# Expert block of a mixture-of-experts kernel: the next block's input transposes stand between the up and the gate products, in place of behind the gate products

## The chip, the cores and the metric

The kernel runs on one core of a Trainium2 chip. The metric is the device time of one execution in microseconds (us); lower is better. The engines are named as the profile names them: PE (TensorE, with PEld for its weight loads), DVE (VectorE), ACT (ScalarE), POOL (GpSimd) and SP (SyncE, which issues most of the DMAs).

## The reference

One layer of a streaming encoder on 2048 prompt tokens and 32 sample tokens of width 1024: a joint projection, a convolution group beside a stick-breaking attention group, an output projection, and then a mixture of 32 experts in 4 groups, of which each token uses two. The change lies in the experts, whose part of the reference is this:

```
def expert_block(args):
    xe, e = args                      # 128 rows of tokens, one expert
    return (jax.nn.silu(xe @ w_g[e]) * (xe @ w_u[e])) @ w_d[e]
yb = lax.map(expert_block, (xb, block_e))
out = zeros.at[row_tok].add(yb * row_w[:, None])
```

xe is 128x1024, w_g and w_u are 1024x512, w_d is 512x1024. Each expert has at least one block of 128 rows; the data of this case gives 46 blocks over 32 experts.

## The kernel before

The program has three stages, each with its own semaphores and a barrier behind it: projection and convolution (names p1_), attention and output projection with the router, and the experts (names p3_, function phase_moe). Only the third is touched. It begins some 1335 us into the span; its blocks run from 1369 us to 2191 us.

All matrices are float32. For precision each operand is kept as a high part (fp32r, written by ACT with a copy) and a low part (the rest, written by DVE with a subtraction), and each product is made of three matmuls: hi x hi, hi x w_lo, lo x w_hi. So one k-tile of 128 rows costs three matmuls.

Work of PE in one block b, in program order (PE runs its instructions in order; each engine has its own stream, ordered by the semaphores that are named):

- up: 8 k-tiles x 3 matmuls of 512 columns into the PSUM tile p_up (L2310, helper `hidden`).
- gate, first half of the columns: 8 x 3 matmuls of 256 columns into p_gp; then five k-tiles of the second half (15 matmuls).
- transpose_h(b, 0): two 128x128 transposes (matmuls against the identity, L2289) of the first half of h, into p_htp.
- the last three k-tiles of the second half of gate (9 matmuls).
- transpose_x(b + 1): eight 128x128 transposes (L2282) of the next block's rows p_xg, into p_xtp.
- down: k-tile 0 of the first 512 output columns (3 matmuls of 512 columns, p_dp, L2301), transpose_h(b, 1) (two transposes), then 21 more matmuls of down.

What stands beside it: ACT's `gate(b, k)` (L2233) makes silu of half k of gate as soon as it is complete (g_done), DVE's `gated(b, k)` (L2441) multiplies it by up into h (h_done), and transpose_h(b, k) waits for that. ACT's `h_hi(b, k)` (L2238) and DVE's `h_rest(b, k)` (L2445) make the high and low part of the transposed h (hl_done), and `down` waits for hl_done[0] before its first matmul and for hl_done[1] before its 13th. ACT's `x_hi(b + 1)` (L2228) and DVE's `x_rest(b + 1)` (L2433) do the same with the next block's x; the next block's up waits for them. ACT's order in a block is: up's weights, gate(b, 0), two weight pieces, h_hi(b, 0), gate(b, 1), x_hi(b + 1), h_hi(b, 1), weights, output of down (L2253), weights. The order of DVE is likewise written out by hand in `block_of`.

Between these, ACT (L2223) and DVE (L2428) split the next expert's weights, which SP loads into a ring of 16 pieces of 512 KB (L2178); this is only done in an expert's last block. POOL gathers the rows of block b + 2 by an indirect DMA into p_xg (L2494), once transpose_x(b + 1) has read the buffer (semaphore xt_ps), and then adds the output of block b into y_out by another (L2504). transpose_x(b) waits for the gather's landing (`gathered`) and for `xl_done`.

The waits at the head of down, in PE's stream, are these:

```
weights(e, 3)
pe.wait_ge(hl_done[0], b + 1)
pe.wait_ge(yo_done, b)
down(0, (0,))
transpose_h(b, 1)
```

Of the kernel before, what the change touches and what calls it, by code (L numbers as in the profile page):

```python
# [2076 lines left out]
def phase_moe(nc, io, scr, picks):  # L2077
# [6 lines left out]
    with ExitStack() as ctx:  # L2084
# [85 lines left out]
        @block.sync  # L2170
        def _(sp):
            def load(i, a):
                for p, src in enumerate(pieces(i * 4 + a)):
                    n = a * PIECES + p
                    if not (isinstance(i, int) and n < RING):
                        sp.wait_ge(wlo_done, i * (4 * PIECES) + n - RING + 1)
                    dst = raw[:, n % RING, :]
                    sp.dma_start(dst.rearrange("p (k f) -> p k f", k=2) if p < 2 * KT // 2 else dst,  # L2178
                                 src).then_inc(raw_in[n % RING], 16)

            sp.wait_ge(zero_yo, 1)
            sp.dma_start(scr["h2"][PAD:ROWS, :], yo[:, :]).then_inc(zeroed, 16)
            sp.dma_start(io["y_out"][PAD:ROWS, :], yo[:, :]).then_inc(zeroed, 16)
            for a in range(4):
                load(0, a)
            with sp.Fori(1, NE // 4) as i:
                for a in range(4):
                    load(i, a)
            sp.wait_ge(zeroed, 32)
# [77 lines left out]
        @block.tensor  # L2267
        def _(pe):
            for n, (k, r) in enumerate(choices):
                m = DEC if ORDER[r] == PT else P  # L2270
                if n in pool_rows:
                    pe.wait_ge(row_in, pool_rows.index(n) + 1)
                pe.wait_ge(spread_in, n + 1)
                pe.matmul(up[:, 0:2 * NBL], homes[n % HOMES][0:m, :],  # L2274
                          in_col[0:m, n % RS, :, :].rearrange("p v b -> p (v b)"),
                          start=(n == 0), stop=(n == len(choices) - 1)).then_inc(spread, 1)

            def transpose_x(b):
                pe.wait_ge(gathered, b * 16)
                pe.wait_ge(xl_done, b)  # L2280
                for k in range(KT):
                    last = pe.transpose(xtp[:, k, :], xg[:, k * P:(k + 1) * P], ident[:, :])  # L2282
                last.then_inc(xt_ps, 1)

            def transpose_h(b, k):
                pe.wait_ge(h_done[k], b + 1)
                for x in range(2):
                    f = 2 * k + x
                    last = pe.transpose(h_cols[k][:, x, :], h[:, f * P:(f + 1) * P], ident[:, :])  # L2289
                last.then_inc(ht_ps[k], 1)  # L2290

            def weights(e, groups):

                pe.wait_ge(whi_done, e * PIECES + groups * 4)
                pe.wait_ge(wlo_done, e * PIECES + groups * 4)

            def down(c, fs):

                for f in fs:
                    for n, (ha, wa) in enumerate(((ht_hi, w_hi), (ht_hi, w_lo), (ht_lo, w_hi))):  # L2300
                        last = pe.matmul(dp[:, c, :], ha[:, f, :], wa[2][:, f, c * 512:(c + 1) * 512],  # L2301
                                         start=(f == 0 and n == 0), stop=(f == FT - 1 and n == 2))
                return last

            def hidden(dst, group, lo, hi, ks):

                for k in ks:
                    for n, (xa, wa) in enumerate(((xt_hi, w_hi), (xt_hi, w_lo), (xt_lo, w_hi))):
                        at = k % 2 * FF
                        last = pe.matmul(dst, xa[:, k, :], wa[group][:, k // 2, at + lo:at + hi],  # L2310
                                         start=(k == 0 and n == 0), stop=(k == KT - 1 and n == 2))
                return last

            for done in (xt_ps, up_done, *g_done, *ht_ps, d_done):
                pe.sem_inc(done, 1)
            def keep_warm(count):

                for _ in range(count):
                    pe.matmul(dp[:, 0, :], w_hi[0][:, 0, 0:P], w_hi[0][:, 0, 0:512], start=True, stop=True)  # L2319

            pe.wait_ge(whi_done, 1)
            keep_warm(22)
            pe.wait_ge(ident_done, 2)
            transpose_x(1)
            keep_warm(8)
            pe.wait_ge(table_done, 1)
            with pe.Fori(0, NE) as e:
                start, end = (pe.value_load(table[0:1, x, bass.ds(e, 1)], min_val=1, max_val=NBL - 2) for x in range(2))
                with pe.Fori(start, end + 1) as b:
                    pe.wait_ge(xh_done, b + 1)  # L2330
                    pe.wait_ge(xl_done, b + 1)
                    weights(e, 1)
                    pe.wait_ge(h_done[1], b)
                    hidden(up[:, :], 0, 0, FF, range(KT)).then_inc(up_done, 1)
                    weights(e, 2)
                    hidden(gp[:, 0, 0:HF], 1, 0, HF, range(KT)).then_inc(g_done[0], 1)
                    hidden(gp[:, 1, 0:HF], 1, HF, FF, range(5))
                    transpose_h(b, 0)
                    hidden(gp[:, 1, 0:HF], 1, HF, FF, range(5, KT)).then_inc(g_done[1], 1)
                    transpose_x(b + 1)  # L2340
                    weights(e, 3)
                    pe.wait_ge(hl_done[0], b + 1)
                    pe.wait_ge(yo_done, b)
                    down(0, (0,))
                    transpose_h(b, 1)
                    down(0, (1,))
                    down(1, (0, 1))
                    pe.wait_ge(hl_done[1], b + 1)
                    down(0, (2, 3))
                    down(1, (2, 3)).then_inc(d_done, 1)  # L2350
# [249 lines left out]
```

## Time and profile before

| | |
|---|---|
| median of 3 runs | 2202.96 us (2202.63 to 2206.08) |
| the profiled execution, its own time | 2202.57 us |
| its span, first to last instruction | 2200.8 us |
| mean granted TensorE clock | 0.977 |
| PE / PEld busy | 2088.1 us (95%) / 1771.5 us (80%) |
| DVE / ACT / POOL busy | 1623.4 / 1260.0 / 806.9 us |
| expert blocks | 46, from 1368.9 us to 2191 us |

The busy time of an engine sums its instructions. PE's matmuls are pipelined and the ends are modelled, so two neighbours overlap in the rows; the distance from start to start says what one costs. A chain of waits follows the work that ended last back from the end. PEldq is PE's sequencer, with its own instructions: semaphore waits (EVENT_SEMAPHORE), register operations and branches. Clock 1.00 is the full 2.4 GHz.

### The profile page before, as it was taken

Reading aid. Unit: us, or ns where it says so; the run is one execution under the profiler, and the core shown is the slowest. Engines: PE = TensorE matmul, PEld = TensorE weight load, DVE = VectorE, ACT = ScalarE, POOL = GpSimd, SP = SyncE. Lnnn points to the kernel's source line nnn. Section 1 sums busy time; section 2 is a strip of 40 time slices with the busy share of each in tenths; the row PEclk is TensorE's granted clock in tenths of the full one; section 3 lists DMA queues with packets and bytes.
Section 4 is the critical chain, followed back from the end, with each engine's and each line's share of the span. In section 5 each row is a group of like instructions: output and inputs, shape, how many; then the busy total and the mean of one; then the engine's idle time right before and its main releaser. Section 6 shows DMA issues by size and latency. Waiting matters only on the chain. (4 is left out here: it accounts for less than half of the span.)

```text
span 2200.8 us, 40164 instructions
## 1 busy us (share of the span) xinstructions
PE 2088.1 (95%) x13505; PEld 1771.5 (80%) x13506; DVE 1623.4 (74%) x2083; ACT 1260.0 (57%) x2200; POOL 806.9 (37%) x689
## 2 busy tenths in 40 slices
PE   8999999995899999899999895999999999999998
PEld 6888888884687887678787774888888888888887
DVE  3799999984777667867878967969698556556644
ACT  5322433335677777866676643768588555456533
POOL 1111544553566654545545435222222222222221
PEclk9999999996999999999999996999999999999999
DMA  7553344334333242333222117989899968767852
GB/s 228 186 191 134 118 128 159 120 106 144 114 117 109 80 131 81 108 105 116 80 73 92 54 70 258 361 281 372 308 357 373 329 197 282 228 198 264 285 172 35
DMA packets 211517, 393.17 MB, mean 179 GB/s; under 512 B 54749, under 2 KB 81757, under 8 KB 211389
## 3 DMA queue, kind: packets, MB, share of 16 engines
q1 hardware_dynamic: 197853, 357.42, 47.1%
q0 software_dynamic: 13536, 34.12, 6.8%
q8 instruction: 72, 1.18, 0.2%
q14 instruction: 56, 0.46, 0.1%
HBM read 315.42 MB, written 91.23 MB: 185 GB/s over the span
## 5 line engine op out<-in xcount | busy, mean ns | idle before, releaser
L2428 DVE TENSOR_TENSOR p_w_lo<-p_raw,p_w_hi 128x1024 fp32r<-128x1024 f32 (+1 forms) x260 | 439.5, 1728 | 150.5 <-ACT p_w_hi L2223 149.9
L2051 POOL TENSOR_TENSOR p_wgt<-p_wgt,p_past 128x1024 f32<-128x1024 f32 (+4 forms) x166 | 308.5, 1859 | 347.2 <-DVE p_past L1929 347.1
L2223 ACT ACTIVATE p_w_hi<-p_raw 128x2048 fp32r<-128x2048 f32 (+1 forms) x198 | 361.8, 1859 | 84.0 <-PE p_up L2310 67.3
L762 DVE SCALAR_TENSOR_TENSOR p_ut<-p_ut,p_cw 128x512 f32<-128x512 f32 (+1 forms) x480 | 329.2, 762 | 0.0
L1929 DVE TENSOR_TENSOR_SCAN p_past<-p_keep,p_past,p_one 128x513 f32<-128x513 f32 (+1 forms) x196 | 225.9, 1193 | 75.3 <-ACT p_keep L1746 73.3
L1746 ACT ACTIVATE p_keep<-p_zp 128x512 f32<-128x512 f32 (+3 forms) x326 | 158.8, 547 | 119.2 <-PE p_zp L1620 106.5
L2310 PE MATMUL p_gp<-p_w_hi,p_xt_hi 128*128 128x256 f32 x736 | 210.4, 286 | 0.0
L436 PE MATMUL p_pj<-p_w_hi,p_xt_hi 128*128 128x512 f32 x512 | 205.2, 401 | 4.2 <-DVE p_xt_lo L738 2.4
L2310 PE MATMUL p_gp<-p_w_lo,p_xt_hi 128*128 128x256 f32 x736 | 206.5, 281 | 0.0
L2310 PE MATMUL p_gp<-p_w_hi,p_xt_lo 128*128 128x256 f32 x736 | 206.4, 280 | 0.0
L436 PE MATMUL p_pj<-p_w_hi,p_xt_lo 128*128 128x512 f32 x512 | 200.6, 392 | 0.0
L436 PE MATMUL p_pj<-p_w_lo,p_xt_hi 128*128 128x512 f32 x512 | 200.2, 391 | 0.0
L2492 POOL COPY p_at_g<-p_slots 128x1 int32 (+1 forms) x47 | 30.8, 656 | 384.8 <-PE p_xtp L2282 382.3
L1759 ACT ACTIVATE p_at<-p_tp 128x512 f32<-128x512 f32 (+3 forms) x261 | 134.2, 564 | 60.3 <-PE p_tp L1630 59.7
L2504 POOL DMA_INDIRECT y_out<-p_yo,p_at_s x47 | 87.8, 1868 | 205.6 <-ACT p_yo L2253 204.7
L1751 ACT ACTIVATE p_wgt<-p_zp 128x512 f32<-128x512 f32 (+3 forms) x326 | 160.3, 562 | 0.0
L1630 PE MATMUL p_tp<-p_ident,p_wgt 128*128 128x128 f32 x1106 | 150.6, 275 | 6.7 <-DVE p_at L1942 5.7
L1658 PE MATMUL p_op<-p_at,p_v 128*64 128x128 f32 x2176 | 156.0, 282 | 0.0
L2301 PE MATMUL p_dp<-p_w_hi,p_ht_hi 128*128 128x512 f32 x368 | 151.1, 411 | 0.4 <-DVE p_ht_lo L2445 0.4
L1929 DVE TENSOR_TENSOR_SCAN p_past<-p_keep,p_one 128x385 f32<-128x385 f32 (+3 forms) x130 | 114.0, 918 | 49.7 <-ACT p_keep L1746 42.8
L2301 PE MATMUL p_dp<-p_w_lo,p_ht_hi 128*128 128x512 f32 x368 | 143.7, 391 | 0.0
L1630 PEld LDWEIGHTS p_tp<-p_ident,p_wgt 128*128 128x128 f32 x1106 | 128.9, 141 | 18.3 <-DVE p_at L1942 6.9
(309 smaller groups left out, 4975.6 us busy)
## 6 DMA issues: line engine op xcount, KB each, us to landing
p_raw<-in_w_up SPq DMA_DIRECT2D x128, 512.0 KB
p_raw<-in_w_gate SPq DMA_DIRECT2D x128, 512.0 KB
p_raw<-in_w_down SPq DMA_DIRECT2D x128, 512.0 KB
wide_raw<-in_w_in SPq DMA_DIRECT2D x56, 256.0 KB, 3.8
wide_raw<-in_x SPq DMA_DIRECT2D x17, 512.0 KB
scr_y<-wide_raw SPq DMA_DIRECT2D x17, 512.0 KB, 3.1
wide_raw<-scr_y SPq DMA_DIRECT2D x17, 512.0 KB
y_out<-wide_raw SPq DMA_DIRECT2D x17, 512.0 KB, 2.9
```

The source lines that it names most:

```text
L436: last = pe.matmul(pj_of(n), xa[:, b, k, :], wa[place[c]][:, k, :], start=(m == 0), stop=(m == 3 * KT - 1))
L762: dve.scalar_tensor_tensor(dst, src, cw[:, a, j:j + 1], dst, ALU.mult, ALU.add).then_inc(tap_done, 1)
L1630: end = pe.transpose(tp[:, n % 2, b * P:(b + 1) * P], wgt[:, u % NW, x * HW + b * P:x * HW + (b + 1) * P], ident[:, :])
L1658: end = pe.matmul(op[x * HD:(x + 1) * HD, pair * P:(pair + 1) * P], v_sb[:, key_slot(g, kt), h * HD:(h + 1) * HD], at[:, (base[u] + x) % N ...
L1746: act.activation(keep_rows[:, u % NK, x, HW - w:HW], zp[:, (base[u] + x) % NZ, 0:w], ACT.Sigmoid, scale=-SCALE).then_inc(keep_done, 1)
L1751: act.activation(wgt[:, u % NW, x * HW:x * HW + w], zp[:, (base[u] + x) % NZ, 0:w], ACT.Sigmoid, scale=SCALE).then_inc(sig_done, 1)
L1929: end = dve.tensor_tensor_scan(past[:, u % NP, to + w + 1:to:-1], src, one[:, 0:1].broadcast_to([P, w + 1]), past[:, (u - 1) % NP, to + 1: ...
L2051: pool.tensor_tensor(mine, mine, past_rows[:, u % NP, 0:n, 2:2 + w], ALU.mult).then_inc(a_done, 1)
L2223: act.activation(part(w_hi, p, wide), raw[:, n % RING:n % RING + wide, :], ACT.Copy).then_inc(whi_done, wide)
L2301: last = pe.matmul(dp[:, c, :], ha[:, f, :], wa[2][:, f, c * 512:(c + 1) * 512], start=(f == 0 and n == 0), stop=(f == FT - 1 and n == 2))
L2310: last = pe.matmul(dst, xa[:, k, :], wa[group][:, k // 2, at + lo:at + hi], start=(k == 0 and n == 0), stop=(k == KT - 1 and n == 2))
L2428: dve.tensor_tensor(part(w_lo, p, wide), raw[:, n % RING:n % RING + wide, :], part(w_hi, p, wide).bitcast(F32), ALU.subtract).then_inc(wlo ...
```

## The change

transpose_x(b + 1) is moved in PE's stream from behind the last gate product to the place between the last up product and the wait for the gate weights. Nothing else is edited: the streams of ACT, DVE, POOL and SP are as they were, and every semaphore is waited for and raised by the same instructions.

```
                     hidden(up[:, :], 0, 0, FF, range(KT)).then_inc(up_done, 1)
+                    transpose_x(b + 1)
                     weights(e, 2)
                     hidden(gp[:, 0, 0:HF], 1, 0, HF, range(KT)).then_inc(g_done[0], 1)
                     hidden(gp[:, 1, 0:HF], 1, HF, FF, range(5))
                     transpose_h(b, 0)
                     hidden(gp[:, 1, 0:HF], 1, HF, FF, range(5, KT)).then_inc(g_done[1], 1)
-                    transpose_x(b + 1)
                     weights(e, 3)
                     pe.wait_ge(hl_done[0], b + 1)
```

## Rows read from the trace of the kernel before

**Rows 1.** The page: the span in 40 equal slices, PE, granted clock and DMA.

```profile
PE   8999999995899999899999895999999999999998
PEclk9999999996999999999999996999999999999999
DMA  7553344334333242333222117989899968767852
```

**Rows 2.** Windows of three blocks: us, busy of each engine, clock, DMA share, GB/s.

```profile
1386.80:1404.66 17.86, 17.86 (x109) 15.91 (x108) 16.26 (x14) 14.40 (x12) 4.96 (x4) 1.00 0.99 324
...
1690.42:1708.96 18.54, 18.10 (x110) 15.94 (x108) 16.17 (x14) 14.64 (x12) 3.67 (x4) 1.00 1.03 367
```

**Rows 3.** The chain that ended last, through one block: start, us, what.

```profile
1637.01 5.44 PE p_up L2310 x24
1642.45 4.59 PE p_gp L2310 x39
1647.04 0.22 PE p_htp L2289 x2
1647.26 1.04 PE p_gp L2310 x9
1648.30 0.87 PE p_xtp L2282 x8
1649.17 0.70 PE p_dp L2301 x3
1649.87 0.22 PE p_gp L2289 x2
1650.09 4.78 PE p_dp L2301 x21
```

**Rows 4.** Timeline of the same block: start, us, engine, instruction.

```profile
1636.84 0.39 PE L2310 MATMUL p_up<-p_w_hi,p_xt_hi 128*128 128x512 f32 x1
...
1639.26 2.00 POOL L2504 DMA_INDIRECT y_out<-p_yo,p_at_s  x1 [3.85 <-ACT p_yo L2253]
...
1647.40 0.37 ACT L2238 ACTIVATE p_ht_hi<-p_htp 128x256 fp32r<-128x256 f32 x1
1647.80 0.43 DVE L2445 TENSOR_TENSOR p_ht_lo<-p_htp,p_ht_hi 128x256 fp32r<-128x256 f32 x1 [0.44 <-ACT p_ht_hi L2238]
1648.02 0.28 PE L2310 MATMUL p_gp<-p_w_hi,p_xt_lo 128*128 128x256 f32 x1
1648.14 1.03 PE L2282 MATMUL p_xtp<-p_ident,p_xg 128*128 128x128 f32 x8
1648.34 0.38 ACT L2233 ACTIVATE p_sg<-p_gp 128x256 f32<-128x256 f32 x1 [0.57 <-PE p_gp L2310]
1648.75 0.42 DVE L2441 TENSOR_TENSOR p_h<-p_up,p_sg 128x256 f32<-128x256 f32 x1 [0.53 <-ACT p_sg L2233]
1648.93 0.48 PE L2301 MATMUL p_dp<-p_w_hi,p_ht_hi 128*128 128x512 f32 x1
1649.43 0.93 POOL L2492 COPY p_at_g<-p_slots 128x1 int32 x1 [8.17 <-PE p_xtp L2282]
1649.71 0.38 PE L2289 MATMUL p_gp<-p_ident,p_h 128*128 128x128 f32 x2
1651.23 1.07 POOL L2494 DMA_INDIRECT p_xg<-scr_h,p_at_g  x1 [0.87 <-POOL p_at_g L2492]
...
1654.70 0.39 PE L2310 MATMUL p_up<-p_w_hi,p_xt_hi 128*128 128x512 f32 x1
```

**Rows 5.** Timeline of the one block whose down products waited.

```profile
1702.52 0.42 DVE L2445 TENSOR_TENSOR p_ht_lo<-p_htp,p_ht_hi 128x256 fp32r<-128x256 f32 x1 [1.32 <-ACT p_ht_hi L2238]
1703.20 0.47 PE L2301 MATMUL p_dp<-p_w_hi,p_ht_hi 128*128 128x512 f32 x1 [0.44 <-DVE p_ht_lo L2445]
1703.96 0.38 PE L2289 MATMUL p_gp<-p_ident,p_h 128*128 128x128 f32 x2
```

**Rows 6.** PE's sequencer in lines 2342 and 2343, 1700 to 1705 us.

```profile
L2342 PEldq EVENT_SEMAPHORE  x1: 51/51/51, 1703.0 to 1703.0; - x1
L2343 PEldq EVENT_SEMAPHORE  x1: 51/51/51, 1703.1 to 1703.1; - x1
```

**Rows 7.** Timeline, attention stage: transposes that waited for a DVE copy.

```profile
554.66 0.41 DVE L1942 COPY p_at<-p_tp 128x256 f32<-128x256 f32 x1
555.13 0.44 PE L1630 MATMUL p_tp<-p_ident,p_wgt 128*128 128x128 f32 x2 [0.29 <-DVE p_at L1942]
```

**Rows 8.** Who waited for whom, 1360 to 2200 us: us, times, longest.

```profile
POOL p_at_g L2492 <- PE p_xtp L2282: 382.3, 46, 10.5
```

**Rows 9.** PE's sequencer at the end of one block, lines 2329 and 2333.

```profile
L2329 PEldq FUSED_REGOPS  x2: 37/39/41, 1651.1 to 1653.4; - x2
L2333 PEldq EVENT_SEMAPHORE  x1: 51/51/51, 1653.7 to 1653.7; - x1
```

**Rows 10.** The instructions of line 2282, all blocks: ns min/median/max.

```profile
L2282 PE MATMUL p_xtp<-p_ident,p_xg x376: 270/272/421, 1364.5 to 2185.4; 128*128 128x128 f32 x188
```

**Rows 11.** DMA queue of the gathers and adds, 1657 to 1658 us: packets, MB, share.

```profile
q0 software_dynamic: 41, 0.09, 24.1%
```

More of the change, by code:

```diff
@@ L2334, in _ @@
                     hidden(up[:, :], 0, 0, FF, range(KT)).then_inc(up_done, 1)
+                    transpose_x(b + 1)
                     weights(e, 2)
@@ L2339, in _ @@
                     hidden(gp[:, 1, 0:HF], 1, HF, FF, range(5, KT)).then_inc(g_done[1], 1)
-                    transpose_x(b + 1)
                     weights(e, 3)
```

## Prediction

> **What bounds the kernel now.** I read the page first, for where PE has holes: in the expert stage, the last third of the slices, PE is busy throughout and its clock is granted in full, while the DMA engines are nearly full up to about 1700 us and less so behind [rows 1]. Then the windows of single blocks: a block lasts 17.86 us and PE is busy for all of it; DVE is busy for 16.2 us, ACT for 14.4 [rows 2]. Then the chain of waits, which settles the bound: it runs through PE alone, from up to gate to transposes to down, and the pieces sum to 5.44 + 4.59 + 0.22 + 1.04 + 0.87 + 0.70 + 0.22 + 4.78 = 17.86 us [rows 3]. So PE never waits in a normal block, and anything that PE does no sooner or that makes it wait is paid once per block, 46 times. One block lasts 18.54 us, 0.68 more; there a weight piece came late and the low part of h with it, and down's first product waited [rows 2, 5].
>
> The last view is the timeline around the edit, because a PE that never waits may do so only since the eight transposes cover something. They do. The last gate product starts at 1648.02. The low part of the transposed h, for which down waits, is done at 1647.80 + 0.43 = 1648.23, which is 0.21 behind that start; the second half of h, for which the next transposes of h wait, is done at 1648.75 + 0.42 = 1649.17, which is 1.15 behind it. The transposes of x fill PE from 1648.14 to 1648.93, so both are ready when PE comes to them, at 1648.93 and 1649.71 [rows 4].
>
> **What the edit removes, adds and moves.** It removes nothing. It moves eight transposes, the two waits ahead of them, and the release that POOL and ACT take from them.
>
> (1) The price of the eight in their new place. Start to start they take 0.79 us (1648.14 to 1648.93) [rows 4], and the chain, which also counts what the first product behind them loses, gives 0.87 [rows 3]. The two transposes of h inside the gate products cost 0.22 in the chain, 0.11 each, so eight ahead of gate products cost 0.88 by the same measure [rows 3]. I take 0.87; 0.79 is the low end. All that stands behind them in the block, gate, silu and h, comes 0.87 later.
>
> A rule speaks against this price. The Trainium skill, page "TensorE: Matmul & The Clock Gate", section "Part 4: PE-mode transpose", gives about 275 ns for a transpose in a kernel; by it the eight would cost 2.2 us in a place where nothing overlaps them, and the kernel would take some 61 us more than by my sum. This trace shows the same length for one transpose, 272 ns at the median, but eight of them in 1.03 us, since they are pipelined [rows 4, 10]; the spacing decides.
>
> (2) What is uncovered. Measured from the start of the last gate product, the transposes of h's second half start now at 1649.71 - 1648.02 = 1.69 us. Without the eight, down would start at 0.12 and these transposes 0.78 behind it (1648.93 to 1649.71), at 0.90 [rows 4]. Two chains hold them back, and neither moves with the eight, for both start from gate products:
>
> - down's first product waits for the low part of h, done at 0.21. Where PE did wait for it, the product started 0.26 behind the end (1702.52 + 0.42 = 1702.94 to 1703.20), as two semaphore instructions of PE's sequencer still stood between [rows 5, 6]. I take 0.25: start at 0.46, and the transposes of h 0.76 behind (1703.20 to 1703.96) [rows 5], at 1.22.
> - the transposes of h wait for h, done at 1.15. How fast that wait lets go is not shown for this line. The nearest row is a transpose that waited for a DVE copy: done at 555.07, started at 555.13, 0.06 [rows 7]. That gives 1.21. The far end is the 0.26 of down's wait: 1.41. I take 0.06, since line 2286 has no semaphore instruction of its own in the sequencer, unlike lines 2342 and 2343 [rows 6]: the wait sits on the transpose itself, as in the attention stage.
>
> The two chains end together, so one stall of about 0.31 us in all (1.22 less 0.90), most of it ahead of down's first product. That the pipe is empty when the transposes start costs a little: two took 0.44 after a wait where two in a flow take 0.38 [rows 4, 7]; I count half of the 0.06, 0.03, as in most blocks this second wait is nearly nil.
>
> (3) The sum for a block: 0.87 + 1.215 - 1.69 + 0.03 = +0.425 us, and 46 x 0.425 = 19.6 us. (Of the 0.425, 0.31 is the stall and 0.03 the refill; 0.08 is what the eight cost beyond their spacing, which the product behind them pays: now gate's first one, while down's first pays as much for the empty pipe.) The block of 18.54 us had a wait of its own in the same place, 0.68 us, from a weight piece that was late. In the new kernel 18 blocks before it are longer by 0.4 us each while the loads are the same, so I count that wait as gone: 19.6 - 0.7 = 18.9. On the profiled execution, span 2200.8 becomes 2219.7 us; what lies around the span (1.8 us) stays, and the median of the runs, 0.4 us above the profiled time, becomes 2202.96 + 18.9 = 2221.9 us.
>
> (4) The rest comes to nothing, with this cover. ACT's high part of the next x starts as soon as silu of the second half is done, no longer after a wait, and its 1.03 us still end before h's second half is transposed, so h_hi(b, 1) isn't later. DVE's low part of that half is done about 1.5 us behind the start of its transposes (1.22 us of weight work stand before it), plus 0.25 for the release, and down needs it 0.14 + 9 x 0.227 = 2.2 us behind them: 0.4 us of slack, and a third stall if that goes. The next x is split 2 us before the block ends. POOL takes its release for the next gather some 5 us earlier in the block, at about 6.5 us instead of 12.6 (1649.43 less the block's start of 1636.8) [rows 4, 8], and its add of the last output is off the engine by then (1639.26 + 2.00, 4.4 us into the block); so the gather and the copy behind it only come earlier. The gather must now have landed 5.7 us into the next block, not 11.3: issue to need stays at 15 us, while the gather issued at 1651.23 shows its packets until 1658 [rows 4, 11]. In the first block alone the issue doesn't move and the cover shrinks to some 6 us, with 4 needed. SP isn't passed; its ring is freed by DVE's weight work, whose pace is set elsewhere.
>
> **Rivals.**
>
> - *The release of h is slow too.* If the transposes of h start 0.26 behind h, they start at 1.41 and the block costs 0.87 + 1.41 - 1.69 + 0.06 = 0.65 us; 46 x 0.65 = 29.9, with the late weight still there: 2233 us. For it: it is the only release of PE in this stage that the trace shows. Against: the missing semaphore instruction.
> - *The sequencer loses its lead.* At an expert's end it needs 2.6 us for its loop (1651.1 to 1653.7) and is done 1.0 us before the next up's first product at 1654.70 [rows 4, 9]. It now gets past down's wait 0.87 later while the block ends 0.43 later, so its lead sinks to about 0.55. If its issue is slower than I take it, each 0.1 us beyond costs 3.2 us over 32 experts; 0.5 beyond gives 2238 us. The Trainium skill, page "Runtime: NRT & Kernel Launch", section "Instruction fetch mechanics", says that a taken branch can force an instruction fetch that stalls; no row here shows such a stall between blocks.
> - *Not slower: the transposes are cheap behind up.* A 512-column product takes 5.44 / 24 = 0.227 us, so 128 columns at that pace take 0.057, and eight transposes 0.45. Then the block costs 0.45 + 1.215 - 1.69 = -0.02 us and the time is 2202 us, the same as now. It decides once the eight cost less than 0.48 us. Against: in all three places of the block they cost 0.11 each [rows 3].
> - *The gather is late.* If landing took 15 us and not 7, each us beyond would cost 46 us. It needs DMA queues much fuller than the trace shows, and I put no size in the range for it.
>
> **How the numbers follow.** The forecast (stall of 0.3 us and nothing hidden) has 0.79; slow release 0.09; sequencer 0.05; cheap transposes 0.03; late gather 0.04. The forecast's own bounds: with the eight at 0.79 and no refill, 0.79 + 1.21 - 1.69 = 0.31 us, 14.3 - 0.7 = 13.6, 2216.5; with the refill in full and the late weight kept, 0.46 x 46 = 21.2, 2224. The range of 8 in 10 takes in most of the slow release: 2214 to 2230 us. Faster or slower by under 0.2% (4.4 us) can't be told from no change. Faster 0.01 (transposes cheaper still, or the late weight's 0.7 us and more), same 0.03, slower 0.96.
>
> **What the profile after would show.** A block period of about 18.28 us. PE idle ahead of p_dp, put down to DVE p_ht_lo, in all 46 blocks, some 0.1 to 0.3 us each, where one stood before; next to none or under 0.1 ahead of the transposes of h. Eight transposes between up and gate, 0.87 us in the chain; ACT p_xt_hi no longer waiting for p_xtp. POOL's copy at 6.5 us into the block. No wait at p_xtp for the gather, and the block near 1690 us like the others. I'm wrong if the period stays at 17.86, which would mean that the eight lost most of their price, or if it is 18.5 or more, where the row ahead of p_gp (L2289) will say whether it was the release of h, or an idle PE ahead of up the sequencer.

## The result and the profile after

The changed kernel is slower: median of six runs 2215.66 us (2213.93 to 2223.40) against 2202.80 us (2199.69 to 2206.08) of six runs of the kernel before. The ratio is 1.0065, 95% interval 1.0046 to 1.0084, so 10.1 to 18.5 us more, 12.9 by the medians. The profiled execution has a span of 2214.1 us, 13.3 more than before.

The chain of waits through one block of the changed kernel, start, us and what; the rows answer to [rows 3]:

```profile
1639.64 5.44 PE p_up L2310 x24
1645.08 0.87 PE p_xtp L2282 x8
1645.95 4.44 PE p_gp L2310 x39
1650.39 0.22 PE p_htp L2289 x2
1650.61 1.06 PE p_gp L2310 x9
1651.67 0.23 issue
1651.90 0.94 PE p_dp L2301 x3
1652.84 0.22 PE p_gp L2289 x2
1653.06 4.78 PE p_dp L2301 x21
```

The block lasts 18.20 us against 17.86. Three things differ, read against [rows 3]. The eight transposes stand ahead of gate at the same price, 0.87. Behind gate there is now "issue" (time in which the chain finds no instruction at work; the timeline below shows PE waiting there for the low part of h), and the three down products behind it have grown from 0.70 to 0.94: together 0.47 us that were not there. And, not foreseen, the 39 gate products take 4.44 in place of 4.59.

The timeline of the same block, behind gate; it answers to [rows 4]:

```profile
1651.22 0.42 DVE L2445 TENSOR_TENSOR p_ht_lo<-p_htp,p_ht_hi 128x256 fp32r<-128x256 f32 x1 [0.52 <-ACT p_ht_hi L2238]
...
1651.39 0.28 PE L2310 MATMUL p_gp<-p_w_hi,p_xt_lo 128*128 128x256 f32 x1
...
1651.71 0.38 ACT L2233 ACTIVATE p_sg<-p_gp 128x256 f32<-128x256 f32 x1 [0.52 <-PE p_gp L2310]
1651.90 0.47 PE L2301 MATMUL p_dp<-p_w_hi,p_ht_hi 128*128 128x512 f32 x1 [0.23 <-DVE p_ht_lo L2445]
...
1652.12 0.43 DVE L2441 TENSOR_TENSOR p_h<-p_up,p_sg 128x256 f32<-128x256 f32 x1 [0.48 <-ACT p_sg L2233]
...
1652.67 0.39 PE L2289 MATMUL p_gp<-p_ident,p_h 128*128 128x128 f32 x2
```

From the start of the last gate product (1651.39): the low part of h is done at 0.25, down starts at 0.51, h's second half is done at 1.16, its transposes start at 1.28. PE now has nothing of its own to do between the last gate product and the first wait. Who waited for whom, 1360 us to the end (us, times, longest), answers to [rows 8]:

```profile
POOL y_out L2504 <- ACT p_yo L2253: 425.1, 46, 11.7
...
POOL p_at_g L2492 <- PE p_xtp L2282: 115.2, 46, 4.7
...
PEld p_dp L2301 <- issue: 15.8, 46, 0.4
PEld p_gp L2289 <- DVE p_h L2441: 12.1, 46, 0.4
...
PE p_dp L2301 <- DVE p_ht_lo L2445: 6.2, 27, 0.3
```

PE's weight loads wait in all 46 blocks at both places, where before down's products had waited once [rows 5]. POOL's wait for the transposes fell from 382 to 115 us, while its wait for the block's output rose from 205 to 425 us and that for the landing of its last add from 5 to 66: the gather is issued earlier and nothing comes of it.

Windows of two blocks of the changed kernel, which answer to [rows 2] (us, busy of PE, PEld, DVE, ACT and POOL, clock, DMA share, GB/s):

```profile
1639.47:1657.67 18.20, 17.98 (x109) 15.73 (x108) 16.17 (x14) 14.40 (x12) 4.64 (x4) 1.00 1.04 382
1493.61:1511.97 18.36, 18.20 (x110) 15.88 (x108) 16.16 (x14) 14.40 (x12) 4.62 (x4) 1.00 1.03 362
```

The granted clock is full (1.00) in both, as before. But blocks come in two lengths. Of the 45 distances between the first up products of neighbouring blocks, 40 are 18.18 to 18.27 us and five 18.36 to 18.38; in those five the 39 gate products took 4.60 us. The chain through one of them:

```profile
1500.09 4.60 PE p_gp L2310 x39
...
1505.96 0.16 issue
1506.12 0.94 PE p_dp L2301 x3
1507.06 0.27 PE p_gp L2289 x2
```

The mean is 18.23 us, 0.354 more than the 17.876 of before (820.37 and 804.42 us over 45 blocks), where 17.876 has the late weight piece of [rows 5] in it. That is 16.3 us over 46 blocks; 3.0 us of it the profiled execution got back ahead of the change, since its first block happened to begin at 1365.91 us and not at 1368.90.

### The profile page after: what moved, and what is told of

Same layout as the page of the kernel before. It is cut to its first block and busy times, and to the rows that moved or that the text cites. A ratio compares the mean times of both kernels' runs of the same rounds, so it can differ in the third digit from the quotient of the medians.

```text
span 2214.1 us, 40164 instructions
## 1 busy us (share of the span) xinstructions
PE 2095.7 (95%) x13505; PEld 1763.0 (80%) x13506; DVE 1622.7 (73%) x2083; ACT 1258.7 (57%) x2200; POOL 807.3 (36%) x689
## 5 line engine op out<-in xcount | busy, mean ns | idle before, releaser
L2310 PE MATMUL p_up<-p_w_hi,p_xt_hi 128*128 128x512 f32 x368 | 143.2, 389 | 0.9 <-DVE p_xt_lo L2433 0.9
L2301 PE MATMUL p_dp<-p_w_hi,p_ht_lo 128*128 128x512 f32 x368 | 144.0, 391 | 0.0
```

## The experiments

The theory, called the cover theory: the transposes behind gate hid two chains, and what is lost is that cover. The rival, called the place theory: transposes cost more between up and gate. In every kernel of these only PE's stream is edited, and the edits are shown against the changed kernel; "period" is the distance from one block's first up product to the next one's. `transpose_x` has got a range of k-tiles; the waits go with its first part, the signal with its last. Where only one execution of a kernel was taken, its period is what is compared, and not its time.

**Four ahead, four behind.**

```
                     hidden(up[:, :], 0, 0, FF, range(KT)).then_inc(up_done, 1)
-                    transpose_x(b + 1)
+                    transpose_x(b + 1, 0, 4, False)
...
                     hidden(gp[:, 1, 0:HF], 1, HF, FF, range(5, KT)).then_inc(g_done[1], 1)
+                    transpose_x(b + 1, 4, KT)
```

> Four of the eight transposes of x between up and gate, four behind gate. Cover theory (the change costs because the two waits, for the low part of h and for h, are no longer covered; they need about 0.4 us of other work behind the last gate product): four transposes behind gate are 0.43 us, so down's first product starts 0.55 us behind the last gate product, no wait shows, and the block period is 17.86 us as before the change, or about 17.70 if the quicker pace of the gate products (0.1135 in place of 0.118 us each) that stands in 40 blocks of the changed kernel comes with any transposes ahead of gate. Time 2203 us, or 2196. Place theory (transposes ahead of gate cost more than behind it, about 1.2 us for eight): half of the loss is left, 18.04 us, time 2209.

Measured: 2205.60 us against 2204.69, ratio 1.0008 (0.9997 to 1.0019). The mean period of the profiled execution is 17.85 us, and the blocks come in two lengths. The chain through two neighbours:

```profile
1601.53 5.44 PE p_up L2312 x24
...
1607.40 4.44 PE p_gp L2312 x39
...
1613.13 0.44 PE p_xtp L2283 x4
1613.56 0.72 PE p_dp L2303 x3
...
1625.18 4.60 PE p_gp L2312 x39
```

Four transposes behind gate are enough to take "issue" out of the chain, and down's first three products are back at 0.7. The period is 17.76 to 17.79 where the 39 gate products take 4.44 us, and 17.91 to 17.94 where they take 4.60. Of the loss of 0.50 us that a block with the long gate has in the changed kernel, 0.07 is left here and not half, so the place theory falls; that the mean period is back at that of before is in part owed to the short gate.

**Six ahead, two behind** (the same edit with 6).

> Six transposes ahead of gate, two behind. Cover theory: the two behind fill 0.22 us of a wait of 0.39, so 0.17 us of waiting is left: period 18.21 - 0.22 = 17.99 us, time about 2206. Place theory: three quarters of the loss, 18.12 us, time 2212.

Measured: 2210.89 us against 2204.69, ratio 1.0032 (1.0021 to 1.0044); the mean period is 18.035, with most blocks at 17.96 to 18.08 and the rest at 18.13 to 18.16. The 17.99 of the cover theory is that of a block with the short gate. The profiled execution took 2206.69 us, about the forecast, though 10 of its 45 blocks had the long gate; it is the fastest of seven, and the median lies 5 us over what I gave. The kernel before stood 2 us higher here as well (2204.69); what the slower executions did otherwise no trace shows.

**The eight in both places.**

```
                     hidden(up[:, :], 0, 0, FF, range(KT)).then_inc(up_done, 1)
-                    transpose_x(b + 1)
+                    transpose_x(b + 1, 0, KT, False)
...
                     hidden(gp[:, 1, 0:HF], 1, HF, FF, range(5, KT)).then_inc(g_done[1], 1)
+                    transpose_x(b + 1)
```

> The eight transposes are done twice, ahead of gate (extra work, its result is overwritten) and behind gate. It gives the price of eight in the new place with the cover kept. Cover theory: no wait; period 17.86 + 0.74 = 18.60 us with the quick gate pace, 17.86 + 0.90 = 18.76 with the slow one; 34 to 41 us over before in all. Place theory: 17.86 + 1.2 = 19.06.

Measured: one execution, 2245.53 us; the period is 18.79 or 18.80 us in every block but the first, 0.93 over the 17.86 of before. The chain:

```profile
1600.83 0.87 PE p_xtp L2283 x8
1601.71 4.60 PE p_gp L2312 x39
...
1607.59 0.88 PE p_xtp L2283 x8
```

No wait, and the same eight transposes cost 0.87 in one place and 0.88 in the other. That is the price of the place by itself: nothing to choose. The other 0.06 of the 0.93 lies in products: gate's last one came 0.90 later and not 0.87, and from the transposes of h to the block's end it took 5.03 us and not 4.99; why, no run shows.

**No transposes but the first block's.** This kernel leaves out the transposes of x for all later blocks, so each computes with the first block's x.

```
-                    transpose_x(b + 1)
+                    pe.wait_ge(gathered, (b + 1) * 16)
+                    pe.wait_ge(xl_done, b + 1)
+                    pe.sem_inc(xt_ps, 1)
```

> Leaves out the transposes of x of all blocks but the first (each block computes with the x of the first one); their waits and their signal stand in the new place. Cover theory: gate loses the 0.79 us that the eight took ahead of it, and the waits behind gate stay as in the changed kernel, 0.38 us in all: period about 18.21 - 0.79 = 17.42, so that leaving out 0.87 us of PE work gains only 0.44 against before. Place theory: no waits that matter, 17.86 - 0.87 = 16.99.

Measured: one execution, 2189.09 us; period 17.44 to 17.51, once 17.59 and once 20.02 (a late weight piece at 1700 us). The chain behind gate:

```profile
1592.49 0.16 issue
1592.65 0.94 PE p_dp L2301 x3
1593.59 0.28 PE p_gp L2289 x2
```

The waits of the changed kernel are here without any transpose ahead of gate. (0.16 and not 0.23 of issue: the low part of h is done 0.18 behind the start of the last gate product here, and not 0.25.) The 39 gate products took 4.59 to 4.60 us in every block. Taking 0.87 us of work off PE shortened the block by 0.40: the rest of the eight's price had been cover.

**Three ahead, five behind.**

> Three transposes ahead of gate, five behind. Cover theory: 0.54 us behind gate cover the wait in full and no instruction of PE is released by another engine; period 17.86 us, or 17.93 if the slow pace behind transposes costs 0.07. On the pace of the gate products, two theories: it is quick (0.1135 us a product) wherever transposes stand ahead of gate: then quick in all or many blocks, 17.77 us; or it can only change where PE is released by another engine's semaphore somewhere in the block AND transposes stand ahead of gate (as the double transposes, with no wait, were slow in every block, and the kernel without transposes, with waits, too): then slow in all blocks, 17.93.

Measured: one execution, 2200.95 us. Cover: as expected, no wait in a normal block. Pace: both theories fell. The first 17 blocks behind the first lasted 17.76 or 17.77 us each; the 19th lasted 21.97, as weights came late and PE waited; behind it nearly all blocks lasted 17.89 to 17.93. The chain before and behind that wait:

```profile
1601.40 4.44 PE p_gp L2312 x39
...
1926.78 4.60 PE p_gp L2312 x39
```

So transposes ahead of gate don't shorten it by themselves, and it can be short with no wait in the block. Here the pace was kept for many blocks; the first block behind the long wait was still short, and from the next one on nearly all were long, so that the wait changed the pace is not shown.

**Five ahead, three behind.**

> Five ahead, three behind. Cover theory: 0.33 us behind gate leave 0.06 us of the wait uncovered: period 17.77 + 0.06 = 17.83 us in blocks with the quick gate pace, 18.00 in those with the slow one; with more than half of the blocks quick the mean is about 17.89, time 2204 to 2205, no difference from before that can be measured.

Measured: 2206.36 us against 2204.34, ratio 1.0009 (1.0000 to 1.0019); periods 17.87 to 17.92 with the short gate, 18.01 to 18.06 with the long one but for the first block, mean 17.954. That is 0.03 to 0.06 over the expectation: the transposes of h start at 1.27 and 1.22 behind the last gate product, about 0.1 of waiting in all.

**Between the halves of gate** (`transpose_x(b + 1)` behind the product that raises g_done[0]).

> The eight stand between the two halves of gate. Cover theory: it does not matter where ahead of the last gate product they stand; the waits behind gate are those of the changed kernel, period 18.2 us (quick pace in the second half) to 18.3 (slow). Place theory (the boundary from up to transposes to gate costs): about 17.9 to 18.0. Pace: the first half of gate, with no transposes ahead of it, stays slow in all blocks; only the second can be quick.

Measured: one execution, 2221.97 us; period 18.32 to 18.38 but for the first block, mean 18.358, at or just above the upper end of what the cover theory gave. The chain:

```profile
1610.43 2.83 PE p_gp L2310 x24
1613.26 0.87 PE p_xtp L2282 x8
1614.13 1.77 PE p_gp L2310 x15
...
1617.17 0.08 issue
1617.25 0.92 PE p_dp L2301 x3
1618.17 0.36 PE p_gp L2289 x2
```

No transposes stand behind up here, and the loss is there all the same, 0.50 us a block. Both parts of gate run at 0.118 us a product in all blocks, the second one too: this is the changed kernel without the shorter gate.

**The first chain started earlier** (the changed kernel, with `range(5)` and `range(5, KT)` of gate's second half made `range(4)` and `range(4, KT)`).

> The changed kernel with the transposes of h's first half three gate products earlier (behind four k-tiles in place of five). Two chains end together in my account: the low part of h for down's first product, and h's second half for the next transposes. If both bind, starting the first chain 0.35 us earlier changes nothing, 18.20 us a block: in blocks without weight work ACT makes the high part earlier and the wait for down's first product shrinks, but the transposes of h then wait for h's second half (1.21 us behind the last gate product); in blocks with weight work ACT is busy with them and the high part comes at the same time as before. If only the first chain counts, the blocks without weight work shorten by 0.2 us to 18.0.

Measured: one execution, 2219.97 us; mean period 18.243. The timeline of a block without weight work:

```profile
1727.65 0.28 PE L2310 MATMUL p_gp<-p_w_hi,p_xt_lo 128*128 128x256 f32 x1
1727.77 0.39 PE L2301 MATMUL p_dp<-p_w_hi,p_ht_hi 128*128 128x512 f32 x1
1727.97 0.38 ACT L2233 ACTIVATE p_sg<-p_gp 128x256 f32<-128x256 f32 x1 [1.03 <-PE p_gp L2310]
...
1728.38 0.42 DVE L2441 TENSOR_TENSOR p_h<-p_up,p_sg 128x256 f32<-128x256 f32 x1 [0.99 <-ACT p_sg L2233]
1728.86 0.44 PE L2289 MATMUL p_gp<-p_ident,p_h 128*128 128x128 f32 x2 [0.25 <-DVE p_h L2441]
```

Down starts 0.12 us behind the last gate product, with no wait at all, and the transposes of h start at 1.21 just the same; the block lasts 18.21. The wait at down is not the bound in such a block, the silu and product of h's second half are. In blocks with weight work the low part of h came nearly as late as in the changed kernel (0.24, down at 0.49), as expected, so of those this run says nothing new. The release is read here as well: h done at 1728.80, transposes at 1728.86, 0.06 us.

**Three ahead, timed, and two ahead.** The split with 3 and with 2, eleven executions of each.

> Three transposes ahead of gate, five behind, timed (its first run was a single look at 2200.95 us, with a block period of 17.77 us up to one late weight piece and 17.91 behind it). If the quick pace of gate is kept wherever nothing makes PE wait, the median should be 2197 to 2200 us, 0.2 to 0.3% under before. If the pace is drawn at random at each wait and then kept, executions differ, from 17.77 to 17.93 us a block, and the median is 2200 to 2207, no measurable difference from before.

> Two ahead, six behind. No wait in any normal block, so the pace of the gate products is the same in all blocks between two late weight pieces: quick (about 17.77 us a block) or slow (about 17.91). Median 2200 to 2206 us; faster than before by 4 us if quick is the common state.

Measured: three ahead 2202.29 us against 2203.50, ratio 0.9995 (0.9984 to 1.0006), no difference; the median that a short gate throughout would give did not come. Its profiled execution had the long gate in nearly all blocks (17.90), where the earlier one had the short one up to the late weights. Two ahead: 2201.00 us, ratio 0.9989 (0.9980 to 0.9998), the only version whose interval lies under the kernel before, and by 0.1%, less than I take for a difference. Against the expectation its pace was not kept: without a wait in it, it went back and forth nearly block by block between 17.77 and 17.89, but for one late weight piece (19.26):

```profile
1605.44 4.59 PE p_gp L2312 x39
...
1623.33 4.43 PE p_gp L2312 x39
```

All periods beside each other, by how many of the eight stand ahead of gate (us; short and long gate: the 39 gate products in about 4.44 or 4.60, one length of 4.59 before):

| ahead / behind | block with short gate | with long gate | waits |
|---|---|---|---|
| 0 / 8 (before) | | 17.86 | none |
| 2 / 6 | 17.77 | 17.89 | none |
| 3 / 5 | 17.77 | 17.90 | none |
| 4 / 4 | 17.77 | 17.93 | none in the chain |
| 5 / 3 | 17.89 | 18.03 | 0.1 |
| 6 / 2 | 18.00 | 18.15 | 0.2 |
| 8 / 0 (changed) | 18.21 | 18.37 | 0.4 |

Up to four ahead the period stands still with the short gate and grows by 0.07 in all with the long one; from there each transpose moved ahead costs its own 0.11 us. That is the shape of a cover of about 0.4 us that is used up.

## Why the prediction was right

The direction, the mechanism and the range held; the size was too large. Forecast were 18.9 us, the medians give 12.9, and 18.9 lies just above the interval (10.1 to 18.5). By its steps:

- *The bound.* PE alone sets the period: doubling eight transposes added 0.93 us per block, and every wait of PE showed up in the period.
- *The price in the new place*, 0.87: 0.87 in the chain, and 0.93 for the block where the cover was kept. What I left out is the pace of the 39 gate products behind them, which in 40 of 45 blocks ran 0.15 us shorter than before. This is the term that was mis-sized: gate's end came 0.74 later in the block and not 0.87. In the other five it came 0.90 later, and they cost 0.50 us more than before; with the pace of before in all blocks the change would have cost 23 us and not 16. Between the halves of gate it did cost 0.50.
- *The two waits.* Forecast from the last gate product: down at 0.46, the transposes of h at 1.21 to 1.22. Measured with the short gate and weight work 0.51 and 1.28, without weight work 0.35 and 1.21; with the long gate 0.44 (0.35 without weight work) and 1.21 to 1.22. So the forecast fits the blocks with the long gate, and a shorter gate gives 0.06 of its 0.15 back at the wait where there is weight work. Which chain binds differs by block: with the short gate and weight work the first (0.51 and the 0.76 from down's start to the transposes make 1.27), else the second, which held at 1.21 when the first was taken away. The forecast had the two end together in every block.
- *The refill*, 0.03, half of 0.06, as the second wait was to be nearly nil in most blocks. In 18 of 45 blocks it was not: two transposes of h took 0.44 there, and from their start to the block's end it was 5.07 us where before it was 4.99, so 0.08. In the others it was 0.02, and 0.045 in the mean.
- *The release of h*, taken as 0.06 by the attention stage's row and not 0.26 by down's: it was 0.06. The rival of a slow release falls.
- *The block with the late weight*, counted as gone: it was gone, no block stands out near 1700 us. That the longer blocks ahead of it did that is not shown. In three kernels with shorter blocks it was longer (20.02 us, 21.97 and 19.26 for blocks of 17.46, 17.77 and 17.8), but with four ahead, and in the timed execution with three ahead, there was none, with blocks of 17.85 and 17.90 us; that it was gone may have been luck.
- *Costed at nothing.* No third stall, none at up beyond a single row at the start, and no wait for the gather at the transposes. The rivals of the sequencer and of the gather did not come true. The cheap transposes did not either: eight were 0.87 behind up too.
- *The sum.* With the late weight counted on both sides, 0.354 measured against 0.41 a block, 16.3 us against 18.9. By its terms, in the mean of the blocks: gate's end 0.76 and not 0.87, the transposes of h 1.26 behind it and not 1.215, the refill 0.045 and not 0.03. The profiled execution's 13.3 us is the 16.3 less 3.0 by which its first block began earlier. That last part is scatter of the stages ahead, which are the same in all these kernels: their first blocks began between 1364.2 and 1371.3 us.

The Trainium skill, page "TensorE: Matmul & The Clock Gate", section "Part 4: PE-mode transpose", gives about 275 ns for one transpose in a kernel, and this case's trace agrees, 272 ns [rows 10]; the 2.2 us for eight, the estimate from that figure for a place without overlap, did not come: behind up they were pipelined as they had been behind gate, 0.87 us.

## What to carry to other kernels

Where one engine sets the period and never waits, ask what each piece of its work covers before moving it: here eight transposes of 0.87 us were work and, for 0.4 us, also the shelter of two chains that run on behind the last gate product. The room can be read beforehand from one timeline: take the moment when each chain ends, add the release, and take off the moment at which its consumer would start without the piece. What is left, 0.3 to 0.4 us here, must stay covered, and only the rest of the piece may be moved, here four of the eight. Moving them gained next to nothing either (0.1% at most, with two), since no wait was to be filled where they went.

## What the runs showed of the hardware that was not expected

The same 39 products of 256 columns, with the granted clock full (1.00), took 4.59 us in every block of before, 4.59 to 4.60 without transposes, and 4.43 to 4.46 or 4.59 to 4.60 with transposes right ahead of them, 0.114 or 0.118 us a product. The program alone does not settle which of the two a block gets: the short one stood in 40 of 45 blocks of the changed kernel, in one of 45 with the transposes in both places, in none with them between the halves, in about every other block with two ahead, and with three ahead in the blocks up to a long wait and in few behind it, while another execution of that kernel had the long one nearly throughout. Two theories on what sets it fell, and the cause stays open. Of the kernel before one execution alone was traced, so whether it ever has the short one is not known. It is worth 0.12 to 0.16 us a block, 6 to 7 us over 46, about half of what this change costs. It may be part of why executions of the split versions scatter over 10 us and more (2193.75 to 2207.44 with three ahead); the kernel before, too, went from 2199.62 to 2209.49 over all its executions.

The two waits of PE let go at different speeds. Down's products started 0.25 to 0.26 us behind the low part of h (1651.64 to 1651.90 here), with two semaphore instructions of the sequencer between, of 51 ns each, as in [rows 6]; the transposes of h, whose wait has no such instruction in the trace, started 0.06 behind h where that wait was the last. That the instructions make the difference is argued from this and was not tested.
